# First pair of an attention in two banks, the next queries behind the scores, and ring places given one by one

## The reference

```python
px = jnp.split(modulate(rms_norm(x, norm1[l]), sh1, sc1) @ w_in[l], splits, axis=-1)
pc = jnp.split(modulate(rms_norm(ctx, norm1[l]), csh1, csc1) @ w_in[l], splits, axis=-1)
k_ctx, v_ctx = _na_heads(pc[1]), _na_heads(pc[2])
na_x = neighbourhood_attention(_na_heads(px[0]), _na_heads(px[1]), _na_heads(px[2]),
                               k_ctx, v_ctx, na_rpb[l])
hg_x, hg_c = hgrn2_mixer(px[3:], pc[3:], lb_all[l], hg_norm[l], need_ctx)
x = x + gt1 * (jnp.concatenate([na_x, hg_x], axis=-1) @ w_out[l])
x = x + gt2 * peer_ffn(modulate(rms_norm(x, norm2[l]), sh2, sc2),
                       peer_wq[l], peer_keys[l], peer_u[l], peer_v[l])
```

```python
q = (t @ wq).reshape(PEER_BLOCK, PEER_HEADS, 2, PEER_DQ // 2)
s = jnp.einsum('tpcd,pckd->tpck', q, sub_keys).astype(jnp.float32)
s1, i1 = lax.top_k(s[:, :, 0], PEER_TOPK)
...
a = jax.nn.gelu(jnp.einsum('tpkd,td->tpk', u[idx], t).astype(jnp.float32), approximate=False)
return jnp.einsum('tpk,tpkd->td', (g * a).astype(t.dtype), v[idx])
```

## Time and profile before

| | us |
|---|---|
| median of 3 runs | 3010.76 |
| lowest and highest run | 3009.21 and 3032.71 |
| the profiled execution | 2999.89 |
| its span in the trace | 2997.7 |

### The profile page before, as it was taken

The page is one execution under the profiler, slowest core; times in us unless marked ns, Lnnn a source line. Parts: engine busy times, 40 slices in busy tenths (PEclk is TensorE's granted clock), DMA queues, the critical chain, the costliest instruction groups (busy, mean ns, idle before and its releaser), DMA issues.

```text
span 2997.7 us, 43889 instructions
## 1 busy us (share of the span) xinstructions
PE 2346.7 (78%) x16542; PEld 1742.9 (58%) x16542; DVE 1922.6 (64%) x4242; ACT 960.7 (32%) x1655; POOL 1072.4 (36%) x1029
## 2 busy tenths in 40 slices
PE   7989988765565544655476989966999999999998
PEld 4767877433411000111274877732777899996998
DVE  3454776786476665566898877763444576666665
ACT  4444654211010000000223433423433545455544
POOL 0000000444456666666666666566454000000000
PEclk8999999887787787776696999977999999999999
DMA  7332114688779999999898999999899345551554
GB/s 290 118 128 77 54 59 169 235 329 313 310 297 374 364 373 370 369 349 363 330 374 299 391 408 408 408 375 341 328 403 387 134 141 192 193 195 62 165 190 145
DMA packets 225234, 810.35 MB, mean 270 GB/s; under 512 B 24704, under 2 KB 30720, under 8 KB 223232
## 3 DMA queue, kind: packets, MB, share of 16 engines
q0 software_dynamic: 147456, 536.94, 46.9%
q1 hardware_dynamic: 77568, 270.61, 25.0%
HBM read 805.35 MB, written 2.10 MB: 269 GB/s over the span
## 4 chain that ended last, share of the span: by engine, by line
PE 38%; DVE 18%; issue 8%; DMA 7%; another core or an unknown queue 7%; POOL 3%; ACT 1%; SPq 0%; DVEq 0%; POOLq 0%; ACTq 0%
PE ps L1851 9%; PE ps L1852 8%; PE ps L1853 8%; DVE pe_ring L2682 6%; PE ps L1791 4%; DMA pe_ring<-in_v,pe_vidx 3%; PE ps L1746 3%; DVE la_w_lo L2730 2%; DMA pe_htok<-in_v,pe_vidx 2%; PE ps L1930 1%; POOL pe_ring L1684 1%; POOL pe_ring L1678 1%; DVE pe_itop L2605 1%; PE ps L1939 1%
## 5 line engine op out<-in xcount | busy, mean ns | idle before, releaser
L1678 POOL DMA_INDIRECT pe_ring<-in_u,pe_idx x419 | 447.7, 1068 | 342.4 <-DVE pe_dots L2682 169.2
L1791 PE MATMUL ps<-pe_ring,pe_spot 128*32 128x512 f32 x1616 | 405.3, 738 | 208.1 <-DMA pe_ring<-in_v,pe_vidx 121.1
L1851 PE MATMUL ps<-la_h_hi,la_w_hi 128*128 128x256 f32 x1856 | 533.8, 288 | 34.2 <-DVE la_w_lo L2730 24.3
L1853 PE MATMUL ps<-la_h_hi,la_w_lo 128*128 128x256 f32 x1856 | 525.8, 283 | 2.9 <-issue 2.9
L1852 PE MATMUL ps<-la_h_lo,la_w_hi 128*128 128x256 f32 x1856 | 526.0, 283 | 0.0
L1684 POOL DMA_INDIRECT pe_ring<-in_v,pe_vidx x404 | 420.2, 1040 | 213.7 <-issue 113.4
L2730 DVE TENSOR_TENSOR la_w_lo<-la_w_raw,la_w_hi 128x1024 fp32r<-128x1024 f32 (+1 forms) x368 | 439.8, 1196 | 77.4 <-ACT la_w_hi L2306 66.5
L2306 ACT ACTIVATE la_w_hi<-la_w_raw 128x1024 fp32r<-128x1024 f32 (+1 forms) x368 | 379.7, 1034 | 313.0 <-DMA la_w_raw<-in_down 84.3
L1851 PEld LDWEIGHTS ps<-la_h_hi,la_w_hi 128*128 128x128 f32 x1856 | 356.8, 192 | 72.4 <-DVE la_w_lo L2730 35.6
L1853 PEld LDWEIGHTS ps<-la_h_hi,la_w_lo 128*128 128x128 f32 x1856 | 354.2, 191 | 0.8 <-issue 0.8
L1852 PEld LDWEIGHTS ps<-la_h_lo,la_w_hi 128*128 128x128 f32 x1856 | 354.3, 191 | 0.5
(11 more groups left out here) (392 smaller groups left out, 3885.6 us busy)
## 6 DMA issues: line engine op xcount, KB each, us to landing
la_w_raw<-in_gate SPq DMA_DIRECT2D x88, 512.0 KB
la_w_raw<-in_up SPq DMA_DIRECT2D x88, 512.0 KB
la_w_raw<-in_down SPq DMA_DIRECT2D x64, 448.0 KB
la_w_raw<-in_a_in SPq DMA_DIRECT2D x40, 512.0 KB
wring<-in_w_in SPq DMA_DIRECT2D x32, 512.0 KB
la_w_raw<-in_down SPq DMA_DIRECT2D x32, 512.0 KB
wring<-in_wq SPq DMA_DIRECT2D x22, 512.0 KB, 8.8
xT<-in_w_mod_rows SPq DMA_DIRECT2D x8, 1024.0 KB, 4.9
```

The source lines that it names most:

```text
L1678: pool.indirect_dma_start(row(n), None, io["u"], bass.IndirectOffsetOnAxis(idx[:, t, j:j + 1], 0)).then_inc(land[GATHERS[n][0]], 16)
L1791: return pe.matmul(ps[PER * grp:PER * grp + PER, half, :], spot[:, j // TOKENS % 2, grp, lo:lo + PER], row(n)[:, half * 512:(half + 1) * 5 ...
L1851: pe.matmul(slot(n), parts_hi[:, n % SPLIT, i, :], hi[:, k, :], start=first, stop=False)
L1853: return pe.matmul(slot(n), w_lo[:, n % RAW, i, :], hi[:, k, :], start=False, stop=last)
```

## The change

It has three parts.

1. **First pair.** Its pieces are made in the order Q, K, KVC, V, then the scores of unit 0, then VT0, VT1, VT2. K, V and VT1 go to bank 6 and the others to bank 7 (`piece_bank`); each waits only for the emptying named in `STAGED_FIRST`, that of the piece two places before it or of the one it reads. On ScalarE, Q's copy stands behind 10 of the 16 conversions, the weight split and K's copy behind the other six, and the negation behind K's copy.
2. **Next queries.** In `PLACE`, Q of the next pair goes behind the scores of a pair's first unit, and VT2 behind the turn; before it was the other way round. In the last pair there is no next Q.
3. **Ring places.** The first gathers take places 0 to 4, 6 to 9, then 5. Places 6 and 7 wait for head 2's products, 8 and 9 for head 3's, and 5 for the last first score; before, all five waited for that score.

```diff
--- before.py
+++ after.py
@@ -248,8 +248,8 @@
 
             PIECES = 7
             Q, K, KVC, V, VT0, VT1, VT2 = range(PIECES)
-            PLACE = {(0, "after_turn"): Q, (1, "after_score"): K, (2, "after_score"): KVC,
-                     (3, "after_score"): V, (3, "after_turn"): VT0, (3, "after_weigh"): VT1, (0, "after_score"): VT2}
+            PLACE = {(0, "after_score"): Q, (1, "after_score"): K, (2, "after_score"): KVC,
+                     (3, "after_score"): V, (3, "after_turn"): VT0, (3, "after_weigh"): VT1, (0, "after_turn"): VT2}
             MARK = {K: 1, KVC: 2, VT0: 3, VT1: 4, VT2: 5}
 
             def piece_at(n, place, do):
@@ -262,6 +262,10 @@
                     do(r, j)
 
             turn_of = {(0, j): j for j in range(PIECES)}
+            STAGED_FIRST = {KVC: Q + 1, V: K + 1, VT0: V + 1, VT1: V + 1, VT2: VT0 + 1}
+
+            def piece_bank(r, j):
+                return ps[:, 6 if r == 0 and j in (K, V, VT1) else 7, :]
 
             def note(r, j):
                 turn_of[r, j] = len(turn_of)
@@ -351,25 +355,28 @@
                         return mm
 
                     def piece(r, j):
-                        if turn_of[r, j]:
+                        bank = piece_bank(r, j)
+                        if r:
                             pe.wait_ge(staged, turn_of[r, j])
+                        elif j in STAGED_FIRST:
+                            pe.wait_ge(staged, STAGED_FIRST[j])
                         if j in (Q, K, V):
                             u = {Q: 0, K: 1, V: 2}[j]
                             if j != V:
                                 pe.wait_ge(split_done[u], splits[u] + r + 1)
-                            mm = three_pass(pe, ps[:, 7, :], u, x_hi, x_lo, (lambda k: pe.wait_ge(rhs_ready, rhs_chunks[0] + k + 1)) if r == 0 and j == Q else None)
+                            mm = three_pass(pe, bank, u, x_hi, x_lo, (lambda k: pe.wait_ge(rhs_ready, rhs_chunks[0] + k + 1)) if r == 0 and j == Q else None)
                             mm.then_inc(projected_ if j == K else mm_done[u], 1)
                         elif j == KVC:
                             pe.wait_ge(split_done[2], splits[2] + r + 1)
                             if r == 0:
                                 pe.wait_ge(rhs_ready, rhs_chunks[0] + 2 * KC)
-                            three_pass(pe, ps[:, 7, 0:L], 1, c_hi, c_lo).then_inc(mm_done[1], 1)
-                            three_pass(pe, ps[:, 7, L:2 * L], 2, c_hi, c_lo).then_inc(projected_, 1)
+                            three_pass(pe, bank[:, 0:L], 1, c_hi, c_lo).then_inc(mm_done[1], 1)
+                            three_pass(pe, bank[:, L:2 * L], 2, c_hi, c_lo).then_inc(projected_, 1)
                         else:
                             tiles = {VT0: range(0, 4), VT1: range(4, 8), VT2: range(8, 10)}[j]
                             for n, t in enumerate(tiles):
                                 c0 = (NA_KC0[t // 2] * NA_KH if t < 2 * BLOCKS else T) + t % 2 * P
-                                mm = pe.transpose(ps[:, 7, n * P:(n + 1) * P], vT[:, c0:c0 + P], ident[:, :])
+                                mm = pe.transpose(bank[:, n * P:(n + 1) * P], vT[:, c0:c0 + P], ident[:, :])
                             mm.then_inc(projected_, 1)
 
                     def score(n):
@@ -434,10 +441,13 @@
                     pe.wait_ge(mod_evac, M_FIRST)
                     mod_sum(M_FIRST - 1, ps[:, 7, 4 * M_FIRST - 4:4 * M_FIRST]).then_inc(mod_summed, 1)
                     pe.wait_ge(gained, 1)
-                    for j in range(PIECES):
+                    for j in (Q, K, KVC, V):
+                        piece(0, j)
+                    score(0)
+                    for j in (VT0, VT1, VT2):
                         piece(0, j)
                     for n in range(UNITS + 2):
-                        if n < UNITS:
+                        if 0 < n < UNITS:
                             score(n)
                         piece_at(n, "after_score", piece)
                         if 1 <= n <= UNITS:
@@ -459,23 +469,24 @@
                         act.activation(hi, src, ACT.Copy).then_inc(rhs_hi_ready, 1)
 
                     def stage(r, j):
+                        bank = piece_bank(r, j)
                         if j in (Q, V):
                             projected(act, {Q: 0, V: 2}[j], r)
                         else:
                             act.wait_ge(projected_, len(MARK) * r + MARK[j])
                         if j == Q:
                             act.activation(qT[:, r % 2, :].rearrange("p (b r i) -> p r b i", b=BLOCKS, i=NA_QB),
-                                           ps[:, 7, :].rearrange("p (r b i) -> p r b i", b=BLOCKS, i=NA_QB), ACT.Copy, scale=-(DH ** -0.5)).then_inc(staged, 1)
+                                           bank.rearrange("p (r b i) -> p r b i", b=BLOCKS, i=NA_QB), ACT.Copy, scale=-(DH ** -0.5)).then_inc(staged, 1)
                         elif j == K:
-                            act.activation(by_column(kT[:, r % 2, 0:T]), by_row(ps[:, 7, :]), ACT.Copy).then_inc(staged, 1)
+                            act.activation(by_column(kT[:, r % 2, 0:T]), by_row(bank), ACT.Copy).then_inc(staged, 1)
                         elif j == KVC:
-                            act.activation(kT[:, r % 2, T:], ps[:, 7, 0:L], ACT.Copy)
-                            act.activation(vT[:, T:], ps[:, 7, L:2 * L], ACT.Copy).then_inc(staged, 1)
+                            act.activation(kT[:, r % 2, T:], bank[:, 0:L], ACT.Copy)
+                            act.activation(vT[:, T:], bank[:, L:2 * L], ACT.Copy).then_inc(staged, 1)
                         elif j == V:
-                            act.activation(by_column(vT[:, 0:T]), by_row(ps[:, 7, :]), ACT.Copy).then_inc(staged, 1)
+                            act.activation(by_column(vT[:, 0:T]), by_row(bank), ACT.Copy).then_inc(staged, 1)
                         else:
                             t0, n = {VT0: (0, 4), VT1: (4, 4), VT2: (8, 2)}[j]
-                            act.activation(v[:, r % 2, t0:t0 + n, :].rearrange("p t n -> p (t n)"), ps[:, 7, 0:n * P], ACT.Copy).then_inc(staged, 1)
+                            act.activation(v[:, r % 2, t0:t0 + n, :].rearrange("p t n -> p (t n)"), bank[:, 0:n * P], ACT.Copy).then_inc(staged, 1)
 
                     def negate(r):
                         act.wait_ge(bias_in[r % 2], 16 * (r // 2 + 1))
@@ -525,15 +536,16 @@
                             for u in range(3):
                                 split_hi(act, parts, u, 0)
                         evac_mod(m, ps[:, m % 4, 0:MODW]).then_inc(mod_evac, 1)
-                    for k in range(KC):
+                    for k in range(KC + 2):
                         high(k)
-                    for k in range(KC, 2 * KC):
+                    stage(0, Q)
+                    for k in range(KC + 2, 2 * KC):
                         high(k)
+                    split_hi(act, parts, 0, 1)
+                    stage(0, K)
                     negate(0)
-                    for j in range(PIECES):
+                    for j in range(KVC, PIECES):
                         stage(0, j)
-                        if j == Q:
-                            split_hi(act, parts, 0, 1)
                     split_hi(act, parts, 1, 1)
                     negate(1)
                     for n in range(UNITS + 2):
@@ -1373,7 +1385,7 @@
 
     def slots_of_gathers():
 
-        free, uses, plan = collections.deque((k, None) for k in range(OUT_RING)), [0] * len(row_spaces), []
+        free, uses, plan = collections.deque((k, None) for k in [*range(FIRST_RING), *range(FIRST_RING + 1, OUT_RING), FIRST_RING]), [0] * len(row_spaces), []
         for n in range(len(ORDER)):
             if n == OUT_FREE:
                 free.extendleft((k, None) for k in range(OUT_RING, RING))
@@ -1663,8 +1675,10 @@
                     pool.wait_ge(h_left, TT - 1)
                 elif OUT_RING <= slot < RING:
                     pool.wait_ge(rest_done, KC)
-                elif FIRST_RING <= slot < OUT_RING:
+                elif slot == FIRST_RING:
                     pool.wait_ge(first_scored, FIRST)
+                elif FIRST_RING < slot < OUT_RING:
+                    pool.wait_ge(first_q, 2 * ((slot - FIRST_RING + 1) // 2))
                 elif n and slot >= RING + 6:
                     pool.wait_ge(dot_done, (slot - RING - 3) * HK)
```

## The result

Over nine runs of each, the kernel before took 3016.99 us in the median (3009.21 to 3032.71) and the changed one 2991.74 (2971.89 to 3006.57). The ratio is 0.9925, 95% interval 0.9900 to 0.9949: 22.6 us less by the ratio (the two medians lie 25.3 us apart), where 20.1 were forecast. The profiled execution of the changed kernel is the quickest of its nine (span 2969.7 us), so the 28.0 us between the two spans are no measure of the change; what can be read from the pair of traces is where each stage begins.

What follows compares the result with a forecast made beforehand. Gathers wait behind attention and the recurrent stage, so attention's savings reach the end: 14.5 + 5.6 + 0 = 20.1 us off the median 3010.8 gives 2990.7, forecast as 2990; range 2977 to 3003, wider 2964 to 3006.

Steps and rivals of the forecast that it cites:

- What bounds the kernel: Whole kernel: gathers stand behind attention and the recurrent stage, so all or nearly all of what attention saves reaches the end.
- One sign of being wrong: Wrong if the time from the recurrent stage's start to the end differs by more than some 5 us from before.
- Part 1: Attention's first pair: 12.7 us from idle before the next Q plus 1.8 us of clock in it, 14.5 us.
- The rebuilding by lengths: First pair: products chained by lengths from the trace, putting the next pair's Q at 74.7 against 87.36 us: 12.7 us.
- The clock: Next pair's Q, behind the chopped transposes: at full clock it takes 5.73 instead of 7.54 us, 1.8 us saved.
- Part 2: Attention units 4, 8 and 12: saves 1.86 and 4.18 us, loses 0.44, in sum 5.6 us.
- Part 3: First gathers: POOL 5.0 us ahead but no one waits for it; zero gain, between -5.0 and +5.0 us.
- POOL's lead: First gathers: four issued 1.24 us apart put POOL 5.0 us ahead, gone from the sixteenth dot on.
- Which are done: First gathers: products of heads 2 and 3 are already done, so four of the five stopped gathers follow at once.
- The long waits: First gathers: ScalarE (8.53 us) and VectorE (10.49 us) wait, unexplained, for TensorE sums that had ended; VectorE's amid full DMA engines.
- The expectation for part 3 in the first conditions: First gathers: ScalarE's first long wait grows by some 3 us, the second shrinks by some 5.6; nothing left at the end.
- The rivals of a caught or a freed head: Routing stage: one 25.39 us TensorE wait more (3021 us, chance 0.08) or one fewer (2965 us, chance 0.12).

Runs made afterwards that it cites:

- part 1, part 2 and both: Kernel before with only the first-pair edits, only the next-queries edits, or both without the ring places: ratios 0.9950, 0.9972 and 0.9920.
- part 3 alone: Kernel before with only the ring places given one by one (`slots_of_gathers` and `slot_free`): ratio 1.0005 (0.9994 to 1.0016).
- the later series: Three later series, twelve runs of variants under other conditions; the kernel before took 2846.23, 2847.46 and 2847.95 us in the median there.
- the later pair: Traces of the unchanged kernel before (2844.35 us) and of the whole change (ratio 0.9935), both run once more under the later conditions.
- before again: The kernel before, unchanged, run once more for its trace under the later conditions: 2844.35 us, one run.
- the change again: The whole change, unaltered, run once more under the later conditions: ratio 0.9935 (0.9917 to 0.9953) to the kernel before.
- with one bank: Changed kernel with all seven pieces of the first pair in bank 7 again, ScalarE's new order kept: 2827.95 us, one run.
- parts 1 and 2 alone: Kernel before with the first-pair and next-queries edits, without the ring places: ratio 0.9920 (0.9903 to 0.9937).

## Why the prediction was right

- **What bounds the kernel** (what attention saves reaches the end): right. The ratios of part 1, part 2 and both give 14, 8 and 23 us of 2846, and their recurrent stage starts 15.4, 8.0 and 22.6 us before that of part 3 alone (238.80), whose attention is that of before. One sign of being wrong did show in the first pair of traces: from the start of the recurrent stage to the end it is 2759.1 us before and 2753.0 with the change, 6.1 apart where 5 was the limit. In the pair of the later series it is 2603.0 and 2602.7, so what attention saves does reach the end.
- **Part 1**, 14.5 us: 15.3 in the first pair of traces (turn of unit 0 at 86.64 for 101.97), 14.1 in the later pair (86.77 for 100.88). The rebuilding by lengths was right to 0.8 us before the next Q (73.86 for 74.7). The missing part: K, KVC and V were given the lengths they have behind a hole. By ScalarE's rows KVC took 64.99 - 59.24 = 5.75 for 6.01 and V 5.47 for 5.73; a product that follows another at once is 0.26 us shorter, as its first matmul starts before the last one of the product before has ended (59.04, where that one runs from 58.81 for 0.39). One reading was wrong: the prediction says that K ran at a granted 1.00 in the kernel before, but most of it ran at 0.50 (the window from 60 to 64 us above). The sum did not suffer, since it gave K the 5.73 us of V; but 2.3 of its 12.7 us are clock and not idle time, and nothing in the prediction says so. And of the sixteen conversions that it calls context conversions, eight are those of the tokens, as the section on the change has it.
- **The clock**, 1.8 us: measured 7.54 - 5.70 = 1.84 in the first pair. This size is partly luck: in before again the clock came back sooner and Q took 93.80 - 87.63 = 6.17, so that only 0.50 was to be had. In every trace with part 1 the next Q took 5.7 us. The Trainium skill, "TensorE: Matmul & The Clock Gate", section "A second HAM failure mode: psum-queue depth-cycling", describes a clock that falls between bursts when work cycles through PSUM banks; by that rule Q would have kept its 7.54. With holes of 0.25 and 0.47 left between bursts, this trace has a granted 1.00 and does not bear it out here.
- **Part 2**, 5.6 us: units 4 and 8 gave 2.08 and 4.39 for 1.86 and 4.18. Unit 12 did not lose its 0.44: without VT2 ahead of it the turn waits 3.03 us instead of 2.66, but from unit 12 to the end of attention it is 0.1 us less in all. In sum 6.6. In the later pair it is 9.2: there unit 4 took 12.52 us before, also at a lowered clock, and gave 3.64, unit 8 gave 4.42, and units 12 to 15 1.17.
- **Part 3**, zero between ends of -5.0 and +5.0: zero is right (1.0005), but the reason was incomplete. The forecast had POOL's lead end at the sixteenth dot. It ends at the twenty-ninth gather, on the wait for the output projection. The lead itself was sized rightly: 28.27 - 23.24 = 5.03 us at the twelfth gather. "Which are done" was wrong for head 3 in the first trace: POOL issued nine gathers in a row there, waited 2.48 us, and issued two more. In the change again it issued all eleven in a row.
- **The long waits.** The expectation for part 3 in the first conditions, one wait longer and the next shorter, fits the one trace (11.41 and 14.13), and by it the changed kernel was 26.35 us ahead at the thirty-third gather and 22.64 at the first. From there on its lead moves between 18 and 30 us and is 25.18 at the last gather, so that this pair does not show whether the 3.7 us were kept or given back. The rivals of a caught or a freed head did not occur. That such waits come with a full DMA, as the earlier trace rows suggested, is refuted as a sufficient cause: before again has the DMA engines full and no such wait. The Trainium skill, "DMA: Bandwidth & Descriptors", section "Queues, rings and completion order", says that a DMA engine takes turns packet by packet between the queues with work. By that rule a backlog slows other transfers and does not hold them, and that trace agrees with it. What held back TensorE's increments in the first series is open; no run of the later series had the waits, so none could take them away.

The forecast of 2990 against a measured 2991.74 is closer than its terms deserve, and that is luck. In the first pair of traces each of the two parts that mattered gave 0.8 and 1.0 us more than forecast. The medians fell by 25.3 us where 20.1 were forecast, and the median of before was 3016.99 over nine runs and not the 3010.76 of three: two errors of 5 and 6 us that nearly cancel.

## What to carry to other kernels

An engine that fills one buffer piece by piece while another empties it loses the emptying each time, and also every delay in the other's queue; and the clock can fall behind the longest hole, which costs as well. A second buffer (with the scores moved) took 13.2 of 13.5 us here, and made the reordering of the other queue (8.8 us by itself) nearly superfluous, so try the buffer first. A lead given to a queue is worth nothing if the same queue waits later for something it does not move: look for the next wait on that queue by another engine before pricing the lead. Holes in one stage are room for independent products of the next stage, and filling them gives back the clock too: in this kernel 48 matmuls there cost nothing, and the first gather came 11 us earlier.

## What the runs showed of the hardware

- The recurrent stage, whose program is the same in all, took 277.4 to 284.4 us from its first product to the first gather in the twelve traces in which it is whole (279.8 in the first trace of before, 277.4 with one bank, 284.4 with part 3 alone). The granted clock in it differs. Here the whole stage, with one bank and then with parts 1 and 2 alone, the same 3043 matmuls in both:

```profile
220.49:497.92 277.43, 248.24 (x3043) 214.79 (x3044) 181.51 (x369) 151.89 (x224) 1.14 (x1) 0.98 0.26 88
216.25:499.84 283.59, 254.00 (x3043) 219.61 (x3044) 181.20 (x369) 151.98 (x224) 1.15 (x2) 0.96 0.25 87
```

  TensorE is busy 5.76 us longer in the second, at a lower mean clock, which is nearly all of the 6.16 us between them; the difference lies in the second half of the stage (granted 0.96 and 0.92 there, 1.00 in both first halves). So two traces can differ by 7 us in a stage that nobody changed. Stages are compared by their starts, and a change of this size by many runs.
- Where POOL did not have to wait, gathers were issued 1.24 us apart in every trace, under both conditions. Of the 155.5 us between the two traces of the kernel before, 129 had come up by the 640th gather (1575.67 and 1446.71 us). They lie in waits, of which those of ScalarE and TensorE above are examples.
